# Splits one unit sooner, fill products, another layout of the modulation product, and one addition moved to GpSimd

## What is computed

```python
def conv_gated_ffn(xn, w_up, conv_w, conv_b, w_down):
    h = causal_depthwise_conv(xn @ w_up, conv_w, conv_b)   # three taps
    a, g = jnp.split(h, 2, axis=-1)
    return (jax.nn.silu(g) * a) @ w_down
...
    # s5_layer: a complex linear recurrence over the tokens
    _, _, xr, xi = lax.associative_scan(_complex_affine_combine, (a_re, a_im, bu_re, bu_im), axis=1)
...
    # second model
    mod = jax.nn.silu(c) @ w_mod[layer] + b_mod[layer]
    mod_c = jax.nn.silu(c_ctx) @ w_mod[layer] + b_mod[layer]
```

## Time and profile before

| what | value |
|---|---|
| median of the runs | 1717.38 us (1717.24 to 1717.69, 3 runs) |
| the profiled execution | 1715.28 us, of it 1713.4 us span |
| TensorE busy | 1650.9 us, 96% of the span, 14840 products |
| VectorE busy | 1239.6 us, 72% |
| ScalarE busy | 852.7 us, 50% |
| GpSimd busy | 104.6 us, 6% |
| granted clock of TensorE, mean | 0.988 |

### The profile page before, as it was taken

How to read it: one execution, slowest core, us unless ns; L and a number is a source line. 1 busy time by engine, 2 the same in 40 slices (tenths; PEclk the granted TensorE clock), 3 DMA queues, 4 the chain that set the end, 5 groups by cost and what they waited for, 6 DMA issues and landing times.

```text
span 1713.4 us, 35193 instructions
## 1 busy us (share of the span) xinstructions
PE 1650.9 (96%) x14840; PEld 1581.9 (92%) x14840; DVE 1239.6 (72%) x1604; ACT 852.7 (50%) x979; POOL 104.6 (6%) x103
## 2 busy tenths in 40 slices
PE   9999999999999997899999999999999999899998
PEld 7989999999999996799999998999998779889998
DVE  6877777897878879857777786777766776654545
ACT  5465554656455541445555546555544644344343
POOL 1001000005400013100000000100000000000000
PEclk9999999999999998999999999999999999999999
DMA  8814555645455534454555781555552123145552
GB/s 324 326 51 171 183 185 176 216 149 188 161 183 183 173 121 150 150 172 151 193 174 176 278 318 65 185 174 178 187 172 99 71 78 99 48 151 187 179 181 90
DMA packets 40647, 286.82 MB, mean 167 GB/s; under 512 B 4640, under 2 KB 4640, under 8 KB 6496
## 3 DMA queue, kind: packets, MB, share of 16 engines
q1 hardware_dynamic: 39600, 280.99, 47.4%
q10 hardware_dynamic: 944, 4.33, 0.7%
HBM read 284.25 MB, written 1.05 MB: 167 GB/s over the span
## 4 chain that ended last, share of the span: by engine, by line
PE 68%; DVE 15%; ACT 9%; issue 7%; DVEq 0%; DMA 0%; ACTq 0%; SPq 0%
PE PS L1948 19%; PE PS L1949 19%; PE PS L1950 19%; ACT whi L414 5%; DVE AR L1255 4%; DVE wlo L1020 4%; ACT AR L531 2%; PE PS L1998 1%; PE PS L2291 1%; PE PS L2308 1%; PE PS L2621 1%; PE PS L2269 1%; PE PS L2661 1%; PE PS L2093 1%; PE PS L2438 0%
## 5 line engine op out<-in xcount | busy, mean ns | idle before, releaser
L1948 PE MATMUL PS<-XH,whi 128*128 128x256 f32 (+1 forms) x2792 | 808.8, 290 | 18.2 <-DVE wlo L1020 8.2
L1949 PE MATMUL PS<-XL,whi 128*128 128x256 f32 (+1 forms) x2792 | 800.5, 287 | 0.0
L1950 PE MATMUL PS<-XH,wlo 128*128 128x256 f32 (+1 forms) x2792 | 800.4, 287 | 0.0
L1020 DVE TENSOR_TENSOR wlo<-raw,whi 128x2048 fp32r<-128x2048 f32 x239 | 548.6, 2297 | 166.0 <-ACT whi L414 165.8
L1948 PEld LDWEIGHTS PS<-XH,whi 128*128 128x128 f32 x2792 | 537.8, 193 | 30.8 <-issue 15.1
L1949 PEld LDWEIGHTS PS<-XL,whi 128*128 128x128 f32 x2792 | 537.9, 193 | 3.7 <-issue 0.5
L1950 PEld LDWEIGHTS PS<-XH,wlo 128*128 128x128 f32 x2792 | 537.8, 193 | 3.3
L414 ACT ACTIVATE whi<-raw 128x2048 fp32r<-128x2048 f32 x239 | 454.4, 1902 | 58.9 <-PE PS L1950 48.9
L1948 PE MATMUL PS<-HH,whi 128*128 128x256 f32 x756 | 215.4, 285 | 8.8 <-DVE wlo L1020 7.0
L1949 PE MATMUL PS<-HL,whi 128*128 128x256 f32 x756 | 214.4, 284 | 0.0
L1950 PE MATMUL PS<-HH,wlo 128*128 128x256 f32 x756 | 214.3, 283 | 0.0
(11 more groups left out here) (392 smaller groups left out, 1496.1 us busy)
## 6 DMA issues: line engine op xcount, KB each, us to landing
raw<-wst SPq DMA_DIRECT2D x247, 1024.0 KB, 4.9
AR<-mst SPq DMA_DIRECT2D x17, 1024.0 KB, 7.4
XT<-x_in SPq DMA_DIRECT2D x2, 512.0 KB, 5.4
raw<-wst SPq DMA_DIRECT2D x2, 512.0 KB, 6.4
AR<-crow ACTq DMA_DIRECT2D x2, 512.0 KB, 6.5
AR<-sbc ACTq DMA_DIRECT2D x1, 1024.0 KB, 6.2
AR<-ctxin ACTq DMA_DIRECT2D x1, 1024.0 KB, 5.8
y_out<-XT SPq DMA_DIRECT2D x4, 256.0 KB, 2.4
```

The lines of the kernel that those rows point to most:

```text
L1020: dve.tensor_tensor(wlo[:, r, :], raw[:, u % RING, :], whi[:, r, :].bitcast(F32), ALU.subtract)\
L1948: pe.matmul(dst, sh, mh, start=first, stop=False, **kw)
L1949: pe.matmul(dst, sh, ml, start=False, stop=False, **kw)
L1950: return pe.matmul(dst, sl, mh, start=False, stop=last, **kw)
```

## The change

It has six parts:

- FFN with convolution: ScalarE and VectorE split unit 3 of the FFN before the work on `up(0)` and unit 4 within it, and all later splits of the FFN come one place sooner. The total number of splits is the same.
- `attention(1)`: VectorE takes the difference for unit 3 inside `scales`, before it copies the row.
- `idle(n)`: n products of 512 bfloat16 columns with a fixed operand into bank 7, whose result nobody reads: 6 before the last `down` of the FFN of layer 3, 11 before the first wait of the last mixer's output projection, 5 and 9 around its last sums.
- Modulation: 16 products of 128 columns for each unit in place of 32 of 64 columns. The two halves of the contraction go to different partitions and are added in the turning product: 8 of those in place of 4.
- The copy of the modulation rows has 1024 columns in place of 512, the addition of the bias is one instruction in place of four.
- State space: GpSimd makes the addition of step s+1 between its two rotation products of step s. VectorE signals after its second product, and waits for the addition before its scans.

```diff
-        MROW = AR[:, 2048:2560]
+        MROW = AR[:, 2048:3072]
+        SEL = SM[:, 256:260]
...
-                for j in range(2):
-                    ahead(u0 + j)
-                    up(j)
+                if conv:
+                    ahead(u0 + 1)
+                    up(0, beside=t.s)
+                    t.s += 1
+                    up(1)
+                else:
+                    for j in range(2):
+                        ahead(u0 + j)
+                        up(j)
...
                 if conv:
                     scales()
-                for j in range(2):
-                    if conv:
-                        take(j)
-                    ahead(u0 + j)
-                    up(j)
+                    take(0)
+                    ahead(u0 + 1)
+                    convolve(0)
+                    take(1)
+                    split_lo(t.s)
+                    t.s += 1
+                    gated(0)
+                    up(1)
...
-                scales()
+                def fourth():
+                    split_lo(t.s)
+                    t.s += 1
+                scales(fourth if i == 1 else None)
...
-                    dve.tensor_tensor(pairs(wk[1]), im, pairs(ts), ALU.mult)
+                    dve.tensor_tensor(pairs(wk[1]), im, pairs(ts), ALU.mult).then_inc(S["bu_mult"], 1)
                     dve.tensor_tensor(pairs(wk[2]), im, pairs(tc), ALU.mult)
                     dve.tensor_tensor(pairs(wk[3]), re, pairs(ts), ALU.mult).then_inc(S["bu_mult"], 1)
-                    dve.wait_ge(S["bu_mult"], s + 1)
-                    dve.tensor_tensor(wk[0], wk[0], wk[1], ALU.add)
+                    dve.wait_ge(S["bu_mult"], 2 * s + 2)
                     dve.tensor_tensor(wk[2], wk[2], wk[3], ALU.subtract).then_inc(S["v_ready"], 1)
-                    dve.wait_ge(S["v_ready"], s + 1)
+                    dve.wait_ge(S["v_ready"], 2 * s + 2)
...
-                for k in range(KT):
-                    for c in range(4):
-                        r, o = 32 * (c ^ (g % 2)), P * (g // 2) + 64 * (c % 2)
-                        mm = pe.matmul(PS[r:r + 32, bank, o:o + 64], SCP[:, k, :],
-                                       raw[:, t.u % RING, k * 256 + 64 * c:k * 256 + 64 * c + 64],
-                                       start=(k == 0), stop=(k == KT - 1))
+                for k in range(4):
+                    for h in range(2):
+                        for c in range(2):
+                            r, o, kh = 64 * h + 32 * c, P * (g % 4), 4 * h + k
+                            mm = pe.matmul(PS[r:r + 32, 6 + g // 4, o:o + P], SCP[:, kh, :],
+                                           raw[:, t.u % RING, kh * 256 + P * c:kh * 256 + P * c + P],
+                                           start=(k == 0), stop=(k == 3))
...
-                for c in range(4):
-                    mm = pe.matmul(PS[:, bank, 8 * c:8 * c + 8], MROW[:, c * P:(c + 1) * P], rows,
-                                   start=True, stop=True)
+                for g in range(8):
+                    mm = pe.matmul(PS[:, 7, 4 * g:4 * g + 4], MROW[:, g * P:(g + 1) * P], SEL, start=True, stop=True)
                 mm.then_inc(S["mod_sum"], 1)
+
+            def idle(n):
+
+                for _ in range(n):
+                    pe.matmul(PS[:, 7, :], IDB[:, :], IDB[:, :].unsqueeze(1).broadcast_to([P, 4, P]),
+                              start=True, stop=True)
...
+                idle(11)
                 pe.wait_ge(S["op_lo"], t.op + 1)
...
+                idle(5)
                 sums(3)
+                idle(9)
...
+            def turned_sum(s):
+
+                wk = W5[s % 2]
+                pool.wait_ge(S["bu_mult"], 2 * s + 1)
+                pool.tensor_tensor(wk[0], wk[0], wk[1], ALU.add).then_inc(S["v_ready"], 1)
+
+            turned_sum(0)
...
                 pool.wait_ge(S["rot_ready"], s + 1)
                 pool.tensor_tensor(wk[1], wk[1], ts, ALU.mult)
+                turned_sum(s + 1)
                 pool.tensor_tensor(wk[3], wk[3], tc, ALU.mult).then_inc(S["x5_ready"], 1)
```

More of the change, by code:

```diff
@@ L578, in ffn @@
                             split_hi(s1 + 2 * (h - n + 1) + j)
-                            up(2 * h + j, beside=s1 + 4 if conv and h == n and j else None)
+                            up(2 * h + j)
                         hidden(h)
+                    split_hi(s1 + 4)
                     if not conv:
-                        split_hi(s1 + 4)
-                    split_hi(s1 + 5)
+                        split_hi(s1 + 5)
                 else:
@@ L1148, in norm_stream, with modulation_rows, modulated @@
                     dve.tensor_tensor(x, x, RSTX.unsqueeze(1).broadcast_to([P, 2, T]), ALU.mult).then_inc(S["normed"], 1)
[L1150 to L1165, removed]
+            def modulation_rows():
+                a, b = (ident[:, 64 * h:64 * h + 64].rearrange("p (c r) -> p c r", r=32)[:, :, 0:2] for h in range(2))
+                dve.tensor_tensor(SEL.rearrange("p (c r) -> p c r", r=2), a, b, ALU.add)
+                dve.tensor_copy(MROW.rearrange("p (a b) -> p a b", a=2), PS[:, 6:8, :]).then_inc(S["mod_rows"], 1)
+            def modulated():
+                dve.wait_ge(S["mod_sum"], 1)
+                add = VEC[:, VC["b_mod"]:VC["b_mod"] + 16]
+                dve.tensor_tensor(MODV[:, 0:16, :], PS[:, 7, 0:32].rearrange("p (j r) -> p j r", r=2),
+                                  add.unsqueeze(2).broadcast_to([P, 16, 2]), ALU.add).then_inc(S["mod_vec"], 1)
             def modulated_gain(i):
@@ L1260, in up, with gated @@
                                 ins.then_inc(S["conv2"], 1)
+                def gated(j, it=None):
+                    k = 0 if it is None else it
+                    bank = PS[:, 4 + (q0 + j) % 2, :].rearrange("p (a b) -> p a b", a=2)
+                    if conv:
                         dve.wait_ge(S["silu_ready"], up0 + j + 1 + 2 * k)
@@ L1277, in hidden, with up @@
                         .then_inc(S["hl_ready"], 1)
+                def up(j, it=None):
+                    convolve(j, it)
+                    gated(j, it)
                 if conv:
                     scales()
-                for j in range(2):
-                    if conv:
-                        take(j)
-                    ahead(u0 + j)
-                    up(j)
+                    take(0)
[6 more added lines that the diff above has]
+                    up(1)
+                else:
+                    for j in range(2):
+                        ahead(u0 + j)
+                        up(j)
                 hidden(0)
@@ L1311, in ffn @@
                             up(2 * h + j)
-                        if conv and h == n:
-                            split_lo(s1 + 4)
                         hidden(h)
+                    split_lo(s1 + 4)
                     if not conv:
-                        split_lo(s1 + 4)
-                    split_lo(s1 + 5)
+                        split_lo(s1 + 5)
                 else:
@@ L1631, in state_space @@
                 dve.wait_ge(S["w_used"], sum(MODS[0]))
[L1632 removed]
+                modulation_rows()
                 lows(3)
@@ L2236, in ffn @@
                     down(n - 1)
+                else:
+                    idle(6)
                 down(n, last=True)
```

27 lines of the change are left out of this document (11 added, 16 removed).

## The result

The changed kernel takes 1705.78 us (median of 4 runs, 1704.92 to 1706.63), the kernel before on the same chip 1717.31 us. The ratio is 0.9934, 95% interval 0.9917 to 0.9951: 11.5 us faster. The forecast was 21.2 us faster, 1696.2 us, and its range ended at 1690 and 1703. The direction was right, the size was off by nearly a half.

The account below looks back on a forecast made before the run. TensorE, busy 96% of the span, was taken as the bound, with VectorE setting the pace in the state space. FFN splits -16.8, start -3.5, fills -2.8, state space with turning +1.9 sum to -21.2 us: 1696.2 us, range 1690 to 1703.

Parts of the forecast that it names:

- The step that failed: FFN loop: VectorE makes up 0.85 us per pass, so hidden pairs are rarely late; only 1.2 and 0.5 us kept back.
- the part on the FFN splits: Four convolutional FFNs: sooner splits remove TensorE's waits for weights, 18.5 us in all; -16.8 us, bounds -18.5 and -12.
- the hidden pair takes the place of the weights: FFNs of layers 1 and 3: wait moves from weights to hidden pair; FFNs -12, total 1701.0 us, chance 0.17.
- Layers 0 and 2: FFNs of these layers: all weight waits go, -2.9 us in layer 0 and -3.1 us in layer 2.
- Start: First attention: unit 3's sooner difference shrinks TensorE's wait (-2.1 us) and keeps the clock full; -3.5 us, bounds -2.1 and -3.8.
- the clock's 1.4 us: Start: the lower clock from 30.4 us on goes because TensorE is busy without a break before it; some 1.4 us.
- Fills: Last mixer: fill products stand inside waits and keep the clock full at two stretches, 1.4 us each; -2.8 us, bounds 0 and -2.8.
- State space: Addition moved to GpSimd costs about +1.1 us at the end; +1.9 us with the turning product.
- GpSimd's meeting: State space steps: GpSimd's last product and VectorE's subtraction and scans wait for each other; +1.05 us, net +0.45 in steps 1 to 7.
- The rule cited there: State space: VectorE instructions with two SBUF inputs and GpSimd reading SBUF block each other, so scans would wait; 1.1 us.
- The turning products: Modulation: 8 turning products in place of 4, in a row of large ones with nothing to hide them; +0.8 us.
- the modulation: Modulation products: as many columns stream as before, beside VectorE's steps, so nothing was taken for it.

Follow-up runs that it names:

- Experiments 4: Changed kernel with one convolution tap instruction of 0.44 us left out of each up in layer 1's FFN, so the result lacks that term; ratio 0.9887 to the kernel before.
- kernel 5: Changed kernel with addition on VectorE, ScalarE's weight copies before the SiLU in layers 1 and 3, layer 3's next-stage split later and no fills there; 1688.0 us.
- kernels 1: Kernel before with only the sooner splits of the four convolutional FFNs; ratio 0.9975, 4.3 us faster than the kernel before.
- 2: Changed kernel with the state space's addition back on VectorE; ratio 0.9922 to the kernel before.
- 3: Changed kernel with ScalarE's weight copies between middle tap and SiLU, reaching layer 3's FFN only; ratio 0.9911 to the kernel before.
- kernel 7: Changed kernel without any of the fill products; ratio 0.9954 to the kernel before.
- experiment 12: Changed kernel without GpSimd's last rotation product in each state space step, so the result lacks it; one run for its trace, no time given.
- Experiment 6: Kernel 5 with VectorE adding the next quarter of the result before the current quarter's low part, behind the FFNs of layers 0 to 2; ratio 0.9823 to the kernel before.
- 11: Kernel before with only unit 3's difference moved inside scales of the first attention; ratio 0.9981, 3.3 us faster than the kernel before.
- 8: Kernel before with the modulation part alone (16 products of 128 columns per unit, eight turning products); ratio 0.9992, 1.4 us faster than the kernel before.
- 10: Experiment 6's kernel with 5 fill products before the last down of layer 3; ratio 0.9818 to the kernel before.
- 9: Kernel 5 with the state space's addition on GpSimd again; ratio 0.9839 to the kernel before.

## Why the prediction was off

**The step that failed** is in the part on the FFN splits: "a hidden pair is in time as long as VectorE begins a pass at most 4 x 5.68 - 16.3 = 6.4 us behind. With 2.9 us put in, it will be over that by 0.3 to 0.5 us two or three times in layer 1, and about once in layer 3", and the -16.8 us that rests on it. It named the right thing that would be late next and priced it at 1.7 us. The runs showed that in layers 1 and 3 VectorE's list is the bound of the whole FFN: 10.7 us to its first take and 181.2 us of list, in the kernel before too. VectorE does not catch up there, as the step has it do: from the end of a hidden pair to that of the next it takes 16.2 us without side work and 18.4 to 19.1 with it, 35.3 us for most pairs of passes in which TensorE needs 34.6. By the forecast's own numbers it would fall back by 2.9 - 2 x 0.85 = 1.2 us in each two passes, and this was not summed over the loop. Its waits for weights in these layers were TensorE waiting for VectorE under another name. Taking them away let TensorE run ahead, until it waited for the same engine at the hidden pairs and before the last down. The two layers gave 3.0 us up to their last down in place of 10.8. Experiments 4 and 5 show it from the other side: only with a shorter list did layer 1's way fall, by 6.3 us both times.

I walked one start and one pass and judged the rest by a margin. The sum over the whole loop would have needed two instructions of the trace of before, the first take and the end of the last pair: 181.8 us, and 10.7 us ahead of it, against the 193.05 us that TensorE took. That leaves 0.5 us to win whatever the splits do, if the list doesn't get shorter; it got 0.5 us shorter, and 1.0 us was won.

**The clock behind the long waits**, 1.6 and 2.2 us, was not in the sum: the forecast spread the hidden pair's waits and had none of 3 to 4 us. It is not certain either: of the six kernels that have layer 1's wait of 2.88 us (the changed one, 1, 2, 3, 7, 12), five have half clock behind it and lose 1.4 to 1.6 us, and kernel 7 has not. The rival "the hidden pair takes the place of the weights" was the right mechanism with the wrong price, -12 for the FFNs in place of -4.3, since it too let the two layers keep half.

**Behind the last down of layers 0 and 2** 1.1 us each was lost, also unforeseen. The difference for the next unit now stands behind the hidden pair, so VectorE's first addition starts 3.0 us behind the start of layer 0's last down (320.08) in place of 1.6 (325.20 before), and the next stage's operand comes from a chain of VectorE and ScalarE of 2.06 us a quarter. Experiment 6 took 0.7 us of each away.

**Layers 0 and 2** themselves: all four waits of each went, as walked, 7.2 us for the forecast's 6.1. VectorE has no side work there. Their way to the last down is 185.7 and 186.2 us, which no later kernel bettered.

**Start**: the wait was right (2.1 us forecast and shown). That the clock's 1.4 us came too is as likely chance: they come and go with the old start as well. Measured alone the whole is 3.3 us, 1.5 to 4.8. **Fills**: right in sum (2.8 forecast, 2.4 by the traces, 3.4 by experiment 7), wrong in place.

**State space**: GpSimd's meeting was forecast in size (1.05 us; 0.97 was shown by experiment 12), in GpSimd's duration, and in its effect on a step (+0.45; 7.91 to 8.25 is +0.34, and 8.90 to 8.31 in step 0 for -0.6). The rule cited there, "Who interferes with whom" of the Trainium skill's page "SBUF — State Buffer", held for the small additions as well: the second of two instructions waits out the first. A scan beside GpSimd is still in no trace. The turning products were right (+0.9 for +0.8). What seems mis-sized is the modulation, taken at nothing since as many columns stream. From one unit behind layer 1's last down to the first unit behind the state space the traces take 104.0 us on average with the old modulation (before, 1, 11), 102.2 with the new one (2, 5, 6, 8, 10) and 104.0 with the new one and the addition on GpSimd (the changed kernel, 3, 4, 7, 9). So the modulation gives some 1.7 us and the move takes some 1.8, but single kernels of a group are up to 3.7 us apart, and the groups overlap. By which mechanism TensorE is done sooner is not shown. That the changed kernel's own trace came out at -0.4 for the +1.9 forecast is in part luck: in the five kernels with this state space the same row is between -0.8 and +2.9, +0.8 on average.

Open: whether the addition is better on either engine, why the eight steps vary by 3 us between kernels that are alike in them, and why the clock falls behind one wait of 2.1 or 2.9 us and not behind another.

## What to carry to other kernels

A wait names what came last, not who is behind, and a busy share of 80% can be a list without slack. Before an order is changed to take a wait away, add up the whole list of the engine that produces it, from its first to its last instruction in the loop, and set it against the consumer's: if the list is as long, the wait will come back under another name, and longer.

If a list is the bound, look for its own small waits in each pass. Two copies moved into another engine's idle time (2.2 us a pass), with the next stage's split moved out of the way in layer 3, gave more than all sooner splits: up to their last downs the four FFNs are 10.2 us shorter than before in the changed kernel and 22.2 us in kernel 5.

A long wait costs more than its idle time where the clock falls behind it. And a gain that one pair of traces shows is not yet the change's: look whether it also stands in a kernel that lacks the edit.

## What the runs showed of the hardware

- The granted clock fell to 0.50 for 3.4 us behind an idle TensorE of 2.9 us (592.6), and for 6.8 us in the stretch around a wait of 4.1 us (1258.2 to 1265.0) though six fill products had ended 4 us ahead of its end. It doesn't always fall: in kernel 7 it stayed full behind the same 2.9 us, and behind the 2.13 us before unit 3 it was 0.51 in before and 1.00 in kernels 1 and 8.
- With 11, 5 and 9 fill products around the waits of the last mixer its two stretches at half clock are in none of nine traces, without them in all of five.
- Two additions of 8 columns on VectorE, with both operands in SBUF, took 1.22 us in place of 0.25 beside a product of GpSimd, which itself took 1.77 us for 1.26. So an instruction of 0.1 us pays for the rest of the other engine's one.
- Eight turning products of 4 columns made the gap between two units 0.9 us longer than four of 8 columns (1.83 us in eleven traces, 0.93 in three): with products as narrow as these their number set the price here, 0.11 us for each of two records, not the columns.
